# A hybrid decoder step: feed-forward products over four PSUM banks of 264 columns each

## What is computed

```python
def swiglu_ffn(h, w_ffn_gate, w_ffn_up, w_ffn_down):
    g = jnp.einsum('btd,df->btf', h, w_ffn_gate)      # 1024 -> 2816
    u = jnp.einsum('btd,df->btf', h, w_ffn_up)        # 1024 -> 2816
    return jnp.einsum('btf,fd->btd', jax.nn.silu(g) * u, w_ffn_down)
    ...
    h = layer_norm(ALPHA * x + mix, ln1_g, ln1_b)
    y = layer_norm(ALPHA * h + swiglu_ffn(h, w_ffn_gate, w_ffn_up, w_ffn_down), ln2_g, ln2_b)
```

## Time and profile before

| what | value |
|---|---|
| median of 3 runs | 2897.59 us (2893.95 to 2899.51) |
| span of the profiled execution (the page gives no other time of it) | 2898.4 us |
| PE busy, PEld busy | 2824.4 us (97%), 2532.0 us (87%) |
| DVE, POOL, ACT busy | 1478.2, 1015.7, 736.7 us |
| L973, share of the chain that ended last | 42% |
| feed-forward products on that chain | 721.12 us, 4464 matmuls |

### The profile page before, as it was taken

How to read it: one execution, slowest core, us unless ns; L and a number is a source line. 1 busy time by engine, 2 the same in 40 slices (tenths; PEclk the granted TensorE clock), 3 DMA queues, 4 the chain that set the end, 5 groups by cost and what they waited for, 6 DMA issues and landing times.

```text
span 2898.4 us, 45631 instructions
## 1 busy us (share of the span) xinstructions
PE 2824.4 (97%) x18894; PEld 2532.0 (87%) x18894; DVE 1478.2 (51%) x2052; ACT 736.7 (25%) x1154; POOL 1015.7 (35%) x603
## 2 busy tenths in 40 slices
PE   8999999999999999999999899999899999999998
PEld 7999999899999985555666699999799999999998
DVE  3535787765666665555444448765652222222226
ACT  2111212353545444454423222010220000000000
POOL 3443333333333323444211124344233333333331
PEclk9999999999999998999999999999899999999999
DMA  4263223564656545222343424353211111111111
GB/s 144 72 199 113 81 89 117 172 182 141 178 155 170 159 119 147 65 61 73 142 173 153 156 91 141 117 180 106 65 37 44 44 46 48 43 43 43 51 51 60
DMA packets 314769, 309.72 MB, mean 107 GB/s; under 512 B 32101, under 2 KB 273002, under 8 KB 312138
## 3 DMA queue, kind: packets, MB, share of 16 engines
q1 hardware_dynamic: 252392, 196.02, 23.8%
q10 hardware_dynamic: 58650, 73.89, 7.5%
q0 software_dynamic: 3584, 37.75, 3.4%
HBM read 229.41 MB, written 78.20 MB: 106 GB/s over the span
## 4 chain that ended last, share of the span: by engine, by line
PE 80%; DVE 12%; ACT 3%; issue 3%; DMA 1%; POOL 1%; ACTq 0%; SPq 0%; DVEq 0%; POOLq 0%
PE ps L973 42%; PE ps L1154 12%; PE ps L1288 4%; DVE cv L2252 3%; PE ps L1312 3%; PE ps L1302 2%; PE ps L1446 2%; PE ps L1402 2%; PE ps L1422 1%; PE ps L1187 1%; PE ps L1191 1%; PE ps L1180 1%; DVE cv L2246 1%; DVE cv L2254 1%; PE ps L937 1%
## 5 line engine op out<-in xcount | busy, mean ns | idle before, releaser
L780 POOL TENSOR_TENSOR whi<-raw,cst 128x1024 fp32r<-128x1024 f32 x160 | 311.9, 1949 | 1144.6 <-PE ps L973 937.4
L782 POOL TENSOR_TENSOR wlo<-raw,whi 128x1024 fp32r<-128x1024 f32 x160 | 433.1, 2707 | 12.6
L973 PE MATMUL ps<-ahi,whi 128*128 128x352 f32 x1728 | 375.7, 325 | 2.1 <-POOL wlo L782 1.4
L973 PE MATMUL ps<-alo,whi 128*128 128x352 f32 x1728 | 375.8, 326 | 0.0
L973 PE MATMUL ps<-ahi,wlo 128*128 128x352 f32 x1728 | 372.2, 324 | 0.0
L973 PEld LDWEIGHTS ps<-ahi,whi 128*128 128x128 f32 x1728 | 294.7, 189 | 2.7 <-POOL wlo L782 1.7
L973 PEld LDWEIGHTS ps<-ahi,wlo 128*128 128x128 f32 x1728 | 296.8, 189 | 0.0
L973 PEld LDWEIGHTS ps<-alo,whi 128*128 128x128 f32 x1728 | 295.6, 188 | 0.0
L1154 PE MATMUL ps<-xhi,whi 128*128 128x352 f32 x768 | 255.9, 333 | 0.4 <-ACT xraw L1764 0.4
L1154 PE MATMUL ps<-xhi,wlo 128*128 128x352 f32 x768 | 247.8, 323 | 0.0
L1154 PE MATMUL ps<-xlo,whi 128*128 128x352 f32 x768 | 247.7, 323 | 0.0
(11 more groups left out here) (368 smaller groups left out, 5031.9 us busy)
## 6 DMA issues: line engine op xcount, KB each, us to landing
raw<-in_w_in SPq DMA_DIRECT2D x61, 512.0 KB, 5.0
s_a<-d_acum SPq DMA_DIRECT2D x32, 512.0 KB, 7.3
d_xbc<-so ACTq DMA_DIRECT2D x24, 528.0 KB, 2.7
gt<-d_g SPq DMA_DIRECT2D x24, 528.0 KB, 3.6
raw<-in_w_ffn_gate SPq DMA_DIRECT2D x22, 512.0 KB, 3.8
raw<-in_w_ffn_up SPq DMA_DIRECT2D x22, 512.0 KB, 3.8
raw<-in_w_ffn_down SPq DMA_DIRECT2D x22, 512.0 KB, 3.5
d_z<-zo ACTq DMA_DIRECT2D x16, 528.0 KB, 5.1
```

The costliest lines, as they stand in the source:

```text
L780: pool.tensor_tensor(whi[s][:, :], raw[:, u], ones[:, 0:1].broadcast_to([P, UNIT]), ALU.mult).then_inc(sem("unit_hi"), k["unit_hi"].adds(1))
L782: pool.tensor_tensor(wlo[s][:, :], raw[:, u], whi[s][:, :].bitcast(F32), ALU.subtract).then_inc(sem("unit_split"), k["unit_split"].adds(1))
L973: last = pe.matmul(ps[0:m, 3 * b + c, 0:width], w(j), x[:, j, at:at + width], start=i == 0, stop=i == n - 1)
```

## The change

From unit 3 of the first block on, the feed-forward products take the tokens in four parts of `QT` = 264 over four banks. Set 0 becomes banks 0 to 3, set 1 banks 4 to 7. ACT and DVE read the sets with `out4` and `quarters` in place of `out3` and `thirds`. Unit 2 keeps three parts. In the last block's token-major product the bank pairs are taken in another order, and the wait for `res_free0` stands ahead of the first tile.

```diff
+QT = TOK // 4
...
+    def out4(b):
+
+        return ps[:, 4 * b:4 * b + 4, 0:QT]
+
+    def quarters(ap):
+        return ap.rearrange("p (c n) -> p c n", c=4)
...
-        def products(b, hi, lo, xh, xl, kt, chunks, m=P, ready=None, between={}):
+        def products(b, hi, lo, xh, xl, kt, chunks, m=P, ready=None, between={}, banks=3):
...
                 for c, (at, width) in enumerate(chunks):
-                    last = pe.matmul(ps[0:m, 3 * b + c, 0:width], w(j), x[:, j, at:at + width],
+                    last = pe.matmul(ps[0:m, banks * b + c, 0:width], w(j), x[:, j, at:at + width],
                                      start=i == 0, stop=i == n - 1)
...
+        in_quarters = [(c * QT, QT) for c in range(4)]
...
-        for u in range(2, 4):
-            dense(u, u % 2, ahi, alo, KT)
-
-        def gate_and_up(ready=None):
+        dense(2, 0, ahi, alo, KT)
+        dense(3, 1, ahi, alo, KT, chunks=in_quarters)
+
+        def gate_and_up():
             for u in range(4):
-                dense(u, u % 2, ahi, alo, KT, ready=ready if u == 0 else None)
+                dense(u, u % 2, ahi, alo, KT, chunks=in_quarters)
...
-                    last = products(e % 2, view(whi[s]), view(wlo[s]), fhi[:, 2 * v:2 * v + 2], flo[:, 2 * v:2 * v + 2], 2, all_tokens)
+                    last = products(e % 2, view(whi[s]), view(wlo[s]), fhi[:, 2 * v:2 * v + 2], flo[:, 2 * v:2 * v + 2], 2, in_quarters, banks=4)
...
-            at, bank = slice(i * P, i * P + n), (6, 0, 2, 4)[i % 4]
+            at, bank = slice(i * P, i * P + n), (0, 2, 4, 6)[i % 4]
...
         pe.wait_ge(sem("unit_split"), k["unit_split"].next())
+        pe.wait_ge(sem("res_free0"), k["res_free0"].next())
         last_half(0, 0)
-        pe.wait_ge(sem("res_free0"), k["res_free0"].next())
         last_half(1, 0)
+        pe.wait_ge(sem("res_free1"), k["res_free1"].next())
         last_half(2, 0)
-        pe.wait_ge(sem("res_free1"), k["res_free1"].next())
         last_half(3, 0)
...
-        def gate(v, j):
+        def gate(v, j, cut=quarters, out=out4):
             act.wait_ge(sem("unit_done"), k["unit_done"].next())
-            act.activation(thirds(fg[j]), out3(0), ACT.Silu).then_inc(sem("res_free0"), k["res_free0"].adds(1))
+            act.activation(cut(fg[j]), out(0), ACT.Silu).then_inc(sem("res_free0"), k["res_free0"].adds(1))
...
-            dve.tensor_tensor(thirds(mm[:, e]), out3(b), thirds(mm[:, e]), ALU.add).then_inc(sem(f"res_free{b}"), k[f"res_free{b}"].adds(1))
+            dve.tensor_tensor(quarters(mm[:, e]), out4(b), quarters(mm[:, e]), ALU.add).then_inc(sem(f"res_free{b}"), k[f"res_free{b}"].adds(1))
...
-                dve.tensor_tensor(thirds(ff[j][:, :]), out3(1), thirds(fg[j]), ALU.mult).then_inc(sem("res_free1"), k["res_free1"].adds(1))
+                dve.tensor_tensor(cut(ff[j][:, :]), out(1), cut(fg[j]), ALU.mult).then_inc(sem("res_free1"), k["res_free1"].adds(1))
```

More of the change, by code:

```diff
@@ L977, in _, with dense @@
         all_tokens = [(c * CH, CH) for c in range(3)]
-        def dense(u, b, xh, xl, kt, wait_free=True, ready=None, between={}):
+        in_quarters = [(c * QT, QT) for c in range(4)]
+        def dense(u, b, xh, xl, kt, wait_free=True, ready=None, between={}, chunks=all_tokens):
             pe.wait_ge(sem("unit_split"), k["unit_split"].next())
@@ L985, in dense @@
             view = lambda t: lambda j: t[:, j * P:(j + 1) * P]
-            products(b, view(whi[s]), view(wlo[s]), xh, xl, kt, all_tokens, ready=ready, between=between).then_inc(sem("unit_done"), k["unit_done"].adds(1))
+            products(b, view(whi[s]), view(wlo[s]), xh, xl, kt, chunks, ready=ready, between=between, banks=len(chunks)).then_inc(sem("unit_done"), k["unit_done"].adds(1))
         uses = [2]
@@ L2092, in _ @@
         for j in range(2):
-            gate(0, j)
+            gate(0, j, thirds, out3)
         with looped(act, (NF - 1) // 2, {k["unit_done"]: 12, k["f_hi"]: 4, k["res_free0"]: 4, k["res_free1"]: 12}):
@@ L2793, in low_part, with hidden @@
             dve.tensor_tensor(flo[:, 2 * v + j], ff[j][:, :], fhi[:, 2 * v + j].bitcast(F32), ALU.subtract).then_inc(sem("f_split"), k["f_split"].adds(1))
-        def hidden(v):
+        def hidden(v, by_thirds=()):
             for j in range(2):
+                cut, out = (thirds, out3) if j in by_thirds else (quarters, out4)
                 dve.wait_ge(sem("unit_done"), k["unit_done"].next(2))
@@ L2818, in down @@
                     low_part(v, 1)
-        hidden(0)
+        hidden(0, (0,))
         low_part(0, 1)
@@ L2835, in normed @@
             n = P if i < 8 else NS
-            bank = (6, 0, 2, 4)[i % 4]
+            bank = (0, 2, 4, 6)[i % 4]
             dve.wait_ge(sem("tile_done"), k["tile_done"].next())
```

## The result

The changed kernel takes 2910.6 us (median of 6 runs, 2905.3 to 2914.2), the kernel before 2895.9 us (median of 6, 2892.3 to 2899.5). The ratio is 1.0046, with a 95% interval of 1.0035 to 1.0058. It is slower by 0.46%, where the prediction had 0.7% faster, and 2.6 us above the top of its range.

A forecast was written before the change was run, and what follows sets the result against it. The prediction took PE's matmul stream in the feed-forward part as the bound. Only the groups of four counted, a gain of 21.2 us, all else at nothing: 2897.6 - 21.2 = 2876.4, say 2876.5 us, range 2856 to 2908.

The forecast's parts named there:

- What bounds the kernel: Feed-forward part runs at the pace of PE's instruction stream, 161.5 ns from one 352-column matmul's start to the next.
- Groups of four, p = 117.5 ns: Feed-forward groups: 5856 matmuls of 264 columns at 117.5 ns take 688.1 us against 709.3, a gain of 21.2 us.
- p: Distance of starts of 264-column feed-forward matmuls: 117.5 ns taken, ends 113.5 and 123.4, equal times at 121.1.
- rival E: Feed-forward matmul pace by chance near break-even, 120.1 to 122.1 ns: 2892 to 2903 us, no change to tell; chance 0.07.
- Rival C: Feed-forward matmuls: step just above 256 columns or odd starts, 122.4 to 123.4 ns, 7.5 to 13.3 us slower; chance 0.20.
- Rival D: Feed-forward matmuls: fixed 14.8 ns plus exact columns, 124.8 ns each, 21.5 us slower, 2919 us; chance 0.06.
- A: The forecast itself: feed-forward matmuls' excess over columns shrinks with width, 115.5 to 120.1 ns, 2865 to 2892 us; chance 0.55.
- The rule of the fixed 2.5 ns: Skill page's rule for warm matmuls: columns at 2.4 GHz plus 2.5 ns; gives 3.7 us more, judged not to fit.
- The loop's five turns add no other wait: PE's feed-forward loop, read from the trace before: no wait beyond 1.4 us for POOL at the start; no size added.
- Clock, "at nothing": PE's granted clock in the feed-forward stage: stays 1.00, PE gapless and the new stream denser; at nothing.
- Reads, weights, entry, exit: Feed-forward stage: DVE and ACT reading sets, POOL's weights, unit 3's start, waits before the token-major product; each at nothing.

The follow-up runs named there:

- run 4: Changed kernel, PE's loop written out, 264 and 256 columns each started every 256 and every 264 columns, output not the layer's: 2906.74 us.
- run 1: Changed kernel with PE's five loop turns written out, so PE never jumps back: 2904.66 us, ratio 1.0022 to the kernel before.
- run 2: Kernel before, parts of 352, with four blocks instead of two in a turn of PE's loop, 1728 matmuls: 2894.3 us.
- run 10: Kernel before with only the last two down results of each turn in four parts of 264, 876 matmuls a turn: 2908.2 us.
- run 12: Kernel before, each turn's last two down results in four parts, 18 matmuls left out per turn (858), output not the layer's: 2878.87 us.
- Run 6: Kernel before with only the down product in four parts of 264, loop kept, 960 matmuls a turn: 2902.59 us, ratio 1.0024.
- run 7: Kernel before with only gate and up in four parts of 264, loop kept, 1056 matmuls a turn: 2908.0 us, ratio 1.0037.
- run 8: Kernel before, thirds of 352, each token part finished over all contraction steps before the next, from unit 2 on: 2888.29 us, ratio 0.9978.
- run 9: Kernel before with parts of 320, 320 and 416, one part at a time over all contraction steps: 2888.73 us, ratio 0.9971.

## Why the prediction was wrong

**What bounds the kernel: right.** The stage ran at the pace of PE's stream in every trace. No read of a set held it up. DVE's idle time ahead of an add didn't shrink from 1.65 to 1.55 us; it is 1.67 in the timeline, since the results come no faster than before.

**Groups of four, p = 117.5 ns: the first step that failed.** It measured 122.0. The step took 256 columns from the earlier trace rows at 113.5 ns, "since 256 is 8 columns away". Those rows are of another product, with `whi` as its moving operand. In `ahi`, 256 columns take 115.8 to 118.9 ns by where they start, and 118.4 at the very starts that the change uses (run 4); with 3.4 ns for eight more columns that is 121.8. The measured value lies within the bounds, 113.5 to 123.4, but the choice between them failed: the neighbour in width wasn't a neighbour in anything else. The idea behind the gain failed with it. What stands over the columns hardly shrinks with the width, 14.8 ns at 352 and 12.0 at 264, so a fourth of them (4 x 12.0 = 48 ns a group) costs more than three wider ones (3 x 14.8 = 44). That is 5.3 us, shown alone by run 1. By itself this would have been near the upper edge of rival E.

**Rival C: right in its time by luck, and in part in its reason.** It gave 2905 to 2911 by a step just above 256 columns or by the starts at 264, from p = 122.4 on. Run 4 shows both: 4.7 ns for going above 256 columns at multiples of 256, and 2.6 for 256 columns that leave those starts. But they don't add up, each is smaller than the 8 ns that C had, and p stayed below its range. Of its +7.5 to +13.3 us the pace explains 5.3; that the measured time fell into its range is owed to the jumps, which it didn't have. Rival D's form, a fixed part beside exact columns, is nearer to the rows from 240 to 320 columns than A's, with about 12 ns for its 14.8. The rule of the fixed 2.5 ns doesn't hold for this stream: the least in `ahi` is 7.1 ns over the columns, in the odd steps of run 4, and the earlier trace rows had 6.8. The Trainium skill, "TensorE: Matmul & The Clock Gate", section "Back-to-back issue gap", gives that rule for a single isolated matmul, which the prediction left out.

**"The loop's five turns add no other wait": the second step that failed.** It was read from the trace of before and carried over to after, without asking what a third more instructions do to a turn. The jumps cost 7.6 us (runs 1, 2, 10 and 12). A turn has 864 matmuls before and 1152 after; the prediction put nothing on that growth and gave no reason for it.

**Clock, "at nothing": failed by 1.5 us.** PE was to be gapless. It had four stops, and after one of them the granted clock was 0.50 until 2582.9 us. Run 6 has one such dip too, run 7 with its shorter stops none, run 10 none with stops of up to 2.1 us, so a stop doesn't bring it every time.

**Reads, weights, entry, exit: right.** No wait of PE for `res_free`, none for POOL behind the stage's first matmul, and the tail from the first 512-column matmul took 48.9 us in both.

The sum was 21.2 us of gain. Corrected: the pace 5856 x (122.0 - 117.5) = 26.4, the jumps 7.6, the clock 1.5, together 35.5; 35.5 - 21.2 = 14.3 of the 14.5 us by which the stage grew.

What stays open: why the excess depends on the start within 256 bytes, why are faster than the same starts in `ahi`, and why one token part at a time is 1.4 to 1.9 ns faster; whether the limit of a turn is its length alone or also where it lies in the 16 KB blocks, since all of these loops begin at nearly the same place of the program.

## What to carry to other kernels

When a change adds instructions inside a hardware loop, count them for one turn and look at the instruction queue of the page: as long as a turn fits, no packet moves after the first turn, and when it doesn't, each jump cost PE 0.8 to 2.1 us here, and half of the change paid most of it. When a pace is read from a neighbouring row, take the row from the same tiles and starts before taking it from the nearest width; 256 columns took 113.5 ns in one place and 118.4 in the other, and the break-even lay only 0.9 ns below what the new pace measured. In a stream of matmuls with weights of their own, finishing one PSUM bank over the whole contraction before the next gained 0.2 to 0.3% here (runs 8 and 9), the only edits here whose time is shown to lie below that of the kernel before.

## What was not expected of the hardware

- 256 columns of the same tile take 113.8 ns or 117.7 ns by 128 bytes of the start, and up to 118.9 in between; a move of 128 bytes swaps the two.
- Eight columns more than 256 cost 8.0 ns where the parts start at multiples of 256 columns, and 3.4 ns, the columns alone, where they start at multiples of 264.
- A turn of 864 matmuls and their loads is fetched once, one of 876 anew each time in packets of 16.3 KB, and the first matmul behind the jump comes 2.6 to 3.1 us after its packet.
- With 352 columns ahead of the jump the stop is 0.97 to 1.44 us from start to start, with 264 columns 1.62 to 2.21 us.
- After a stop of 2.0 us (start to start) the clock fell to 0.50 in the changed kernel, and after one of 2.2 us in the same trace it didn't.
- The order of the same matmuls is worth 1.4 to 1.9 ns each: 160.1 and 159.6 ns for 352 columns instead of 161.5.
